# A hybrid decoder step on one core: the sample tokens' small products placed among the products of the half gates

## What is computed

```python
q, k, v, u, cq, gates = _split_in(x @ w_in[l])      # gates: sigmoid of 3 x 1024 columns
o_a = _swa_prompt(q, k, v, sinks)                   # prompt: 128-blocks, 16 heads, 4 kv heads, sinks
o_c = _cross_attend(cq, mk, mv)                     # prompt: 4 heads into 256 memory rows

# sample tokens: the same against cached keys and values, per sequence
o_a, kk, vv = _swa_sample(q, k, v, cache_win_k[l], cache_win_v[l], sinks[l])   # 8 x 128 cached rows
o_c = _cross_attend(cq, cache_mem_k[l], cache_mem_v[l])                        # 8 x 256 cached rows

m = gates[..., 0, :] * (o_a @ wa) + gates[..., 1, :] * (o_b @ wb) + gates[..., 2, :] * (o_c @ wc)
h = _layer_norm(ALPHA * x + m @ wo, g1, b1)
out = _layer_norm(ALPHA * h + _hier_moe(h, ...), g2, b2)
```

## Time and profile before

| what | value |
|---|---|
| three runs | 886.21, 890.83, 892.33 us (median 890.83, mean 889.8) |
| the profiled execution | 887.14 us, its span 885.0 us |
| TensorE busy | 834.8 us, 94% of the span |
| VectorE, ScalarE, GpSimd busy | 59%, 49%, 19% |
| chain of work that ended last | TensorE 88%, VectorE 5%, DMA 3% |
| attention loop | from about 161 to 314 us of the span |

### The profile page before, as it was taken

One profiled execution on the slowest core, in us unless ns is written; L12 is line 12 of the kernel. 1 busy time (PEld: TensorE's weight loads), 2 busy tenths in 40 slices (PEclk: granted clock), 3 DMA queues, 4 the chain that ended last, 5 costly groups with the idle time before them and its releaser, 6 DMA issues.

```text
span 885.0 us, 13927 instructions
## 1 busy us (share of the span) xinstructions
PE 834.8 (94%) x5436; PEld 736.4 (83%) x5436; DVE 525.3 (59%) x709; ACT 435.5 (49%) x578; POOL 164.7 (19%) x145
## 2 busy tenths in 40 slices
PE   8999988998998999999999996599999999999994
PEld 7999987787887899999998775587888888888882
DVE  4222155546446353333335434689999999999977
ACT  4222222556455442222224114277888788778864
POOL 0194013222122200000000145411121111111002
PEclk9999999999999999999999999599999999999998
DMA  9322200841022032222224255799999999999973
GB/s 329 132 89 95 95 26 24 296 158 48 26 96 90 1 100 100 99 99 90 89 95 153 68 192 179 294 420 398 399 401 396 378 401 400 401 377 399 400 200 96
DMA packets 38287, 179.80 MB, mean 203 GB/s; under 512 B 3935, under 2 KB 11775, under 8 KB 24126
## 3 DMA queue, kind: packets, MB, share of 16 engines
q1 hardware_dynamic: 32630, 159.22, 47.1%
q0 software_dynamic: 5600, 19.99, 8.1%
q10 hardware_dynamic: 16, 0.03, 0.0%
HBM read 164.65 MB, written 16.89 MB: 205 GB/s over the span
## 4 chain that ended last, share of the span: by engine, by line
PE 88%; DVE 5%; DMA 3%; issue 1%; ACT 1%; DVEq 0%; SPq 0%; POOL 0%; POOLq 0%; ACTq 0%
PE ps L1212 7%; PE ps L1593 7%; PE ps L1213 7%; PE ps L1594 6%; PE ps L1595 6%; PE ps L1214 6%; PE ps L1084 5%; PE ps L1085 5%; PE ps L1086 4%; PE ps L1620 3%; PE ps L1622 3%; PE ps L1621 3%; PE ps L1228 2%; PE ps L1300 2%; PE ps L1427 2%; PE ps L1230 2%
## 5 line engine op out<-in xcount | busy, mean ns | idle before, releaser
L2098 DVE TENSOR_TENSOR elo<-eraw,ehi 128x2048 fp32r<-128x2048 f32 x96 | 218.0, 2290 | 25.9 <-ACT ehi L907 24.0
L907 ACT ACTIVATE ehi<-eraw 128x2048 fp32r<-128x2048 f32 x96 | 183.0, 1916 | 27.8 <-PE ps L1595 16.6
L1593 PE MATMUL ps<-ehi,xethi 128*128 128x512 f32 x256 | 103.1, 403 | 4.0 <-issue 2.7
L1594 PE MATMUL ps<-ehi,xetlo 128*128 128x512 f32 x256 | 101.0, 394 | 0.0
L1595 PE MATMUL ps<-elo,xethi 128*128 128x512 f32 x256 | 100.9, 394 | 0.0
L1212 PE MATMUL ps<-xhi,whi 128*128 128x260 f32 x256 | 73.7, 288 | 0.0
L1084 PE MATMUL ps<-xhi,whi 128*128 128x260 f32 x256 | 72.3, 283 | 0.0
L1085 PE MATMUL ps<-xhi,wlo 128*128 128x260 f32 x256 | 72.3, 282 | 0.0
L1213 PE MATMUL ps<-xhi,wlo 128*128 128x260 f32 x256 | 72.2, 282 | 0.0
L1214 PE MATMUL ps<-xlo,whi 128*128 128x260 f32 x256 | 72.2, 282 | 0.0
L1086 PE MATMUL ps<-xlo,whi 128*128 128x260 f32 x256 | 72.1, 282 | 0.0
(11 more groups left out here) (382 smaller groups left out, 2084.6 us busy)
## 6 DMA issues: line engine op xcount, KB each, us to landing
eraw<-w_gate_in SPq DMA_DIRECT2D x32, 1024.0 KB, 19.3
eraw<-w_up_in SPq DMA_DIRECT2D x32, 1024.0 KB, 19.5
eraw<-w_down_in SPq DMA_DIRECT2D x32, 1024.0 KB, 21.4
raw<-wz_in SPq DMA_DIRECT2D x7, 1024.0 KB, 5.1
late<-wm_in SPq DMA_DIRECT2D x8, 896.0 KB, 4.5
late<-wm_in SPq DMA_DIRECT2D x7, 704.0 KB, 4.0
fraw<-wm_in SPq DMA_DIRECT2D x8, 512.0 KB, 3.6
late<-wo_in SPq DMA_DIRECT2D x4, 1024.0 KB, 5.0
```

What stands on the lines that cost most here:

```text
L907: ac.activation(ehi[s % 3][:, :], eraw[s][:, :], ACT.Copy).then_inc(ehi_ok, 1)
L1593: pe.matmul(ps[:, bank, :], hi[:, k, :], ehi[s[j]][:, w], start=k == 0, stop=False)
L1594: pe.matmul(ps[:, bank, :], lo[:, k, :], ehi[s[j]][:, w], start=False, stop=False)
L2098: ve.tensor_tensor(elo[s % 3][:, :], eraw[s][:, :], ehi[s % 3][:, :].bitcast(F32), ALU.subtract)\
```

## The change

The sample tokens' scores (steps 1 to 12) and cached window values (steps 8 to 11) leave the block between the prompt's values and the half gate. They now stand inside the half gate of the same step, one product behind every triple: the four scores behind triples 0 to 3, the four values behind triples 4 to 7. The waits that the scores had (for `kt_ok`, and in step 1 `qs_ok` and `row_out`) move to just ahead of the half gate. ScalarE's copy `scol` in step 4 gets a wait for `ks_ps`. No product is added or taken away. The core of the diff:

```diff
+                    ac.wait_ge(ks_ps, 4)
                     ac.activation(scol[:, :], ps[:, 7, 0:P + NS], ACT.Copy).then_inc(sw_act, 1)
...
                     if among is not None:
-                        memory_values(among, k)
+                        small(among, k)
...
+            def small(i, q):
+
+                if 1 <= i <= NKT and q < 4:
+                    sample_scores(i - 1, q)
+                if S_PV <= i <= S_OUT and q >= 4:
+                    window_values(i, q - 4)
+                if M_PV <= i <= M_OUT:
+                    memory_values(i, q)
 
             def sample(i):
 
-                if 1 <= i <= NKT:
-                    sample_scores(i - 1)
...
-                if S_PV <= i <= S_OUT:
-                    for p in range(2):
...
                 if i < NKT:
                     sample_keys(i)
+                if 1 <= i <= NKT:
+                    score_waits(i - 1)
...
                 if fill_after(g) is not None:
-                    fill(fill_after(g), g if M_PV <= g <= M_OUT else None)
+                    fill(fill_after(g), g)
```

More of the change, by code:

```diff
@@ L1318, in sample_keys, with score_waits @@
                 last.then_inc(kt_ps, 1)
-            def sample_scores(n):
+            def score_waits(n):
                 pe.wait_ge(kt_ok, n + 1)
@@ L1326, in sample_scores @@
                     pe.wait_ge(row_out, 3)
[L1327 to L1335, removed]
@@ L1336, in sample_scores @@
-                last.then_inc(ks_ps, 1)
+            def sample_scores(n, u):
+                if n < 4:
+                    b, p = 2 * n + u // 2, u % 2
+                    out = ps[:, 7, 64 * p:64 * p + 64].rearrange("q (a b j) -> q a b j", a=2, b=NS)[:, :, b, :]
+                    last = pe.matmul(out, kt[:, u * P:u * P + P], qsp[:, p, :, b, :], start=True, stop=True)
+                else:
+                    b, k, t = n - 4, u // 2, u % 2
+                    out = ps[:, 3, 32 * k + 16 * t:32 * k + 16 * t + 16].rearrange("q (a b) -> q a b", a=2)[:, :, b]
+                    last = pe.matmul(out, kt[:, u * P:u * P + P], cqp[:, t, :, b], start=True, stop=True)
+                if u == 3:
+                    last.then_inc(ks_ps, 1)
@@ new lines, in window_values @@
+            def window_values(i, u):
+                b, p = 2 * (i - S_PV) + u % 2, u // 2
+                out = ps[:, 7, 3 * P + 64 * p:3 * P + 64 * p + 64].rearrange("q (a b j) -> q a b j", a=2, b=NS)
+                prob = pcol[:, 64 * p:64 * p + 64].rearrange("q (a b j) -> q a b j", a=2, b=NS)
+                last = pe.matmul(out[:, :, b, :], cach_v[:, b, p * P:p * P + P], prob[:, :, b, :],
+                                 start=False, stop=b == NS - 1, skip_group_check=True)
+                if i == S_OUT and u == 3:
+                    last.then_inc(sw_ps, 1)
```

## The result

The changed kernel takes 904.98 us (median of four executions, 902.14 to 906.18), the kernel before beside it 888.78 us (886.21 to 892.33). The ratio is 1.0163, interval 1.0132 to 1.0195. That is slower by 1.6%, outside the predicted range of 891 to 902 us. The profiled execution took 904.09 us, 17.0 us more than that of before.

A forecast was written before the change was run, and what follows sets the result against it. TensorE, busy 88% of the last chain, was taken to set the end. Order +6.8 us, called +7, and clock zero, on the three runs' mean of 889.8, gave 897 us; 8 in 10 range 891 to 902 us.

The forecast's parts named there:

- The sum of the order: Steps 1 to 12: moved products cost odd steps 0.88 to 1.76 us each, even steps gain 0.2 us together; +6.8 us.
- the term of the clock: Attention loop: slow stretches at half clock change by zero net, with -1.5 us and +4.5 us as ends.
- the price of a stretch: Half gate of step 8 takes 4.50 us instead of 2.95 at half clock, so a stretch costs 1.5 us.
- the fewer from the one and the more from the other: Fewer slow stretches from step 8's split run of small products, more from 1.6 to 2.1 us waits in six odd steps.
- Step 8's fall: Half clock at 228 to 230 us, read as following small products without any wait; 1.5 us.
- The clock falls in more of the odd steps: Rival, chance 0.18: three more stretches in odd steps at 1.5 us each on top of +7; 901.5 us.
- 1.18 us in step 7: Wait for VectorE's `sstat` in step 7, said to leave the clock whole; evidence against the rival of more clock falls.
- The lone small product: Rival, chance 0.07: a small product behind a triple is nearly free; 890 us, or 882.6 us if wholly hidden.
- the half gate does not start sooner: Denies a rival, chance 0.08: odd half gates start sooner, held by TensorE's order and not `flo`; 889.5 us.
- The merge weights: Transfers after step 11: 1.5 us of slack stay, no cost; rival that they come late, chance 0.04, 899 us.
- ScalarE's `kt` copy: Ahead of `pt` of step 4: half a microsecond later, covered by idle time, which also grows by 0.88 us.

The follow-up runs named there:

- tail version: Changed kernel with the small products as one block behind the half gate's last triple, in odd and even steps: 893.75 us, 1.0042 against the kernel before.
- late version: Changed kernel with all small products behind triples 4 to 7 of the half gate: 894.8 us, 1.0048 against the kernel before.
- head_block: Changed kernel with the small products as one block behind the half gate's waits, ahead of its first triple: 905.26 us, 1.0181 against the kernel before.
- mid_hifirst: Changed kernel, `fhi` products first; odd steps' block between them and the `flo` wait, even steps and step 7 keeping theirs: 883.29 us, 0.9932 against before.
- late_9_11: Changed kernel with the four scores behind triples 4 to 7 in steps 9 and 11 alone: 905.15 us, 1.0156 against the kernel before.

## Why the prediction was wrong

**The sum of the order was right.** One small product costs 0.23 us among the triples (I had 0.22), the odd half gates start where `flo` lets them, the waits grew by 7.0 us, and steps 1, 3 and 5 come out to 0.03 us. Steps 9 and 11 without the clock's part, as in the tail version, take 9.50 and 9.94 us; I had 9.53 and 9.96. Over the timed executions the order costs 6.3 us by span times clock. That the tail and the late version are only 0.4 and 0.5% slower, some 4 us, is clock in their favour: 0.970 and 0.968 granted against 0.967 of before, whose executions also include nine of 48 at 892 us and more.

**The step that failed is the term of the clock: "I take zero, with -1.5 us and +4.5 us (three more) as ends."** It measured +10.9 us in the profiles, 9.4 us in the mean of the timed executions, and 1.2% between the changed kernel and the tail version. Two things in it were wrong. First the price of a stretch: I read 1.5 us from step 8 of before. In the changed kernel one fall cost 3.0 us in step 7, and 3.0 + 1.7 in steps 9 and 10, because the clock stayed low for the rest of the half gate and into the next step. Then the number: I let the fewer from the one and the more from the other cancel. But what went was one fall (1.6 us in step 8), and what came were waits of 1.5 to 2.2 us in six odd steps, each now followed by small products. That mixing takes a run of small products apart I counted as a help. It was none: putting them behind the wait was the harm, and it was the same whether they stood mixed or as one block (`head_block`).

**Step 8's fall was not what I read in it.** I took it for one that follows small products without any wait. In each of the 17 profiles one fall begins in step 7 or step 8, never one in each. Where step 7 waits 2.2 us (ten profiles) it is always step 7. Where it waits 1.2 us it is step 7 in five, at 10.3 us instead of 8.75, and step 8 in two, before and `mid_hifirst`. So the fall at 228 us is more likely step 7's, come later, than one of step 8's own; why it comes later in two of seven is not shown.

**The rival was right in kind.** "The clock falls in more of the odd steps", 0.18 and 901.5 us, is what happened, at 904.98 us; with the profiles' 10.9 us it would have been 889.8 + 7 + 11 = 908. Its evidence against, that 1.18 us in step 7 left the clock whole, was one execution: five of the seven profiles with that wait lost it there.

**The other terms.** The lone small product is not free, the half gate does not start sooner. The merge weights were no matter: the last piece was issued at 272.16, took 6.7 us and was split at 283.15, 4.3 us of slack; I had 1.5, and the rest is there because the slow clock held back the split as well. ScalarE's `kt` copy in step 3 was late and its idle time grew, as told: `pt` of step 4 starts 1.07 us after the transposes, before 1.08.

```profile
192.30 0.60 ACT L814 ACTIVATE pt<-ps 128x512 f32<-128x512 f32 x1 [1.77 <-PE ps L1440]
...
272.16 0.41 SPq L485 DMA_DIRECT2D first<-wm_in  x1
...
283.15 1.90 ACT L776 ACTIVATE whi<-first 128x2048 fp32r<-128x2048 f32 x1
```

**Open.** What precisely the chip answers to is not settled. Shown is that the extra loss needs both, the long waits and small products early behind them: taking away either over all odd steps takes it away. Single falls need neither: before has two of them, one in step 8 and one in step 13, behind a wait with no moved product. And in step 7 of the changed kernel and step 9 of `late_9_11` the clock was down before the first small product. So the small products can't have started those two falls. That they make a stretch longer, and more falls likely in the steps that follow, would fit all versions, but no run separates it from other readings. That it is the share of real work over a stretch is argued, not shown.

## What to carry to other kernels

Cover taken from a wait can cost more than the wait's growth: where thin work, products of few columns, follows the grown wait (1.5 to 2.2 us here), TensorE may run on at half clock, and that cost more here (9.4 us) than the order itself (6.3 us). Before moving filler, ask whether the wait can be made needless; here the products that need only the ready half of the weights go first, which gave 1% whichever way the small ones stood. And don't hunt such a loss in the step where one profile shows it: a second profile of the same kernel had it elsewhere. The granted clock of every timed execution tells order from clock sooner than any one profile.

## What the runs showed that I had not expected

- A fall of the clock has no fixed price. In the same kernel it cost 1.5 us where the products were dense (step 13: 9.71 us, 8.20 in the second profile), 3.0 to 4.7 us where small ones were mixed in (steps 7, 9 and 10), but also 1.5 us with small ones mixed in (step 5 of the second profile, 10.78 us instead of 9.24).
- Small products of 2 or 8 columns among triples cost nothing in the even steps (0.9975), and 1.9%, the order's part in it, when only the odd ones have them, with waits of 1.5 to 2.2 us.
- At half clock a triple with its small product takes 1.08 us instead of 0.57, and eight transposes 1.95 us instead of 1.04.
- Two executions of the same program lost the same share (0.91 over the loop) in different steps.
